# An expert loop one step shorter, with the last item's rows summed in by one-hot products

## The reference

```python
# 64 routed experts, the best 8 for each token, and one shared expert
gates = sel / jnp.sum(sel, axis=-1, keepdims=True) * ROUTED_SCALE
...
h = jax.nn.silu(xb @ w_gate[e]) * (xb @ w_up[e])
y = (h @ w_down[e]) * g[:, None]
return acc.at[tok].add(y), None
...
x = layer_norm(DEEPNORM_ALPHA * x + ffn, ln2_g[l], ln2_b[l])
```

## Time and profile before

| what | value |
|---|---|
| median of 3 runs | 1369.25 us (1366.78 to 1371.58) |
| the profiled execution | 1365.46 us, span 1363.9 us |
| PE busy | 1293.6 us, 95% of the span |
| DVE, ACT, POOL busy | 954.3, 792.3, 483.7 us |
| DMA | 324.11 MB, mean 238 GB/s |
| chain, by engine | PE 81%, DVE 8%, DMA 5%, issue 2%, ACT 2%, POOL 1% |

### The profile page before, as it was taken

The page is one execution under the profiler, slowest core; times in us unless marked ns, Lnnn a source line. Parts: engine busy times, 40 slices in busy tenths (PEclk is TensorE's granted clock), DMA queues, the critical chain, the costliest instruction groups (busy, mean ns, idle before and its releaser), DMA issues.

```text
span 1363.9 us, 25482 instructions
## 1 busy us (share of the span) xinstructions
PE 1293.6 (95%) x6257; PEld 1069.0 (78%) x6258; DVE 954.3 (70%) x1115; ACT 792.3 (58%) x1045; POOL 483.7 (35%) x441
## 2 busy tenths in 40 slices
PE   7989888899989999999999999999999999999966
PEld 6877776788867888888888888888888888888852
DVE  5989977766664958575796456646669579777737
ACT  4122266222255959575786556656678678676724
POOL 0000115366553334334344334334334343333422
PEclk9999879899998999999999999999999999999998
DMA  6121304232569999897999698869889899999747
GB/s 250 47 93 47 144 11 139 89 90 79 160 197 336 356 327 309 301 281 247 338 343 350 211 260 276 264 193 306 286 270 368 249 335 338 339 328 305 216 121 306
DMA packets 78065, 324.11 MB, mean 238 GB/s; under 512 B 22656, under 2 KB 24864, under 8 KB 52816
## 3 DMA queue, kind: packets, MB, share of 16 engines
q1 hardware_dynamic: 43152, 251.05, 49.1%
q0 software_dynamic: 33728, 68.47, 21.4%
q10 hardware_dynamic: 1152, 4.19, 0.8%
HBM read 290.51 MB, written 67.72 MB: 263 GB/s over the span
## 4 chain that ended last, share of the span: by engine, by line
PE 81%; DVE 8%; DMA 5%; issue 2%; ACT 2%; POOL 1%; ACTq 0%; POOLq 0%; SPq 0%; DVEq 0%
PE ps L1813 37%; PE ps L1831 18%; PE ps L1550 6%; PE ps L1678 5%; PE ps L1586 4%; DMA raw<-in_w_up 3%; PE ps L1757 2%; PE ps L1564 2%; DVE cv L1118 2%; PE ps L1844 1%; PE ps L1669 1%; PE ps L1598 1%; PE ps L1642 1%; POOL list_d L600 1%; PE ps L1745 1%
## 5 line engine op out<-in xcount | busy, mean ns | idle before, releaser
L1813 PE MATMUL ps<-wgu,xTe 128*128 x2304 | 548.8, 394 | 3.8 <-issue 2.5
L1813 PEld LDWEIGHTS ps<-wgu,xTe 128*128 128x128 f32 x2304 | 425.7, 188 | 90.7 <-issue 5.8
L653 POOL DMA_INDIRECT sum_d<-ysb,idx x95 | 177.7, 1870 | 508.5 <-ACT ysb L918 438.6
L1831 PE MATMUL ps<-wdn,hT 128*128 (+1 forms) x1236 | 299.3, 391 | 0.0
L1421 DVE TENSOR_TENSOR wgu<-raw,wgu (+1 forms) x128 | 287.7, 2289 | 6.0 <-issue 2.3
L1831 PEld LDWEIGHTS ps<-wdn,hT 128*128 128x128 f32 x1236 | 232.3, 189 | 48.3 <-DVE wdn L1354 0.2
L841 ACT CAST wgu<-raw (+1 forms) x128 | 246.8, 1929 | 3.1 <-SPq L450 2.5
L1426 DVE TENSOR_TENSOR xTe<-ps,xTe 128x512 fp32r<-128x512 f32 x194 | 124.6, 684 | 138.0 <-ACT xTe L910 138.0
L918 ACT ACTIVATE ysb<-ps,idx 128x512 f32<-128x512 f32 x188 | 119.1, 685 | 122.6 <-PE ps L1831 122.6
L1421 DVE TENSOR_TENSOR wdn<-raw,wdn x64 | 146.7, 2293 | 59.5 <-ACT wdn L903 59.1
L643 POOL DMA_INDIRECT xg<-x_d,idx x99 | 110.1, 1113 | 45.1 <-issue 34.3
(11 more groups left out here) (231 smaller groups left out, 1185.3 us busy)
## 6 DMA issues: line engine op xcount, KB each, us to landing
raw<-in_w_gate SPq DMA_DIRECT2D x64, 1024.0 KB, 11.4
raw<-in_w_up SPq DMA_DIRECT2D x64, 1024.0 KB, 8.4
raw<-in_w_down SPq DMA_DIRECT2D x64, 1024.0 KB, 9.4
wraw<-in_w_in SPq DMA_DIRECT2D x10, 512.0 KB, 3.4
xin<-in_xt SPq DMA_DIRECT2D x8, 512.0 KB, 7.6
wraw<-in_w_kv SPq DMA_DIRECT2D x8, 512.0 KB, 3.3
wor<-in_w_out SPq DMA_DIRECT2D x4, 1024.0 KB, 7.9
xres<-in_x SPq DMA_DIRECT2D x8, 512.0 KB, 4.9
```

The costliest lines, as they stand in the source:

```text
L653: g.indirect_dma_start(out=sums, out_offset=bass.IndirectOffsetOnAxis(ap=idx[:, c % RING, c % 2:c % 2 + 1], axis=0), in_=ysb[:, c % 2], in ...
L1813: last = mm(ps[:, 2 + s, :], xTe[:, s, st, d], wgu[:, w, mo, d].rearrange("p a n -> p (a n)"), start=(d == 0 and st == 0 and mo == 0), sto ...
L1831: last = mm(ps[:, down_bank(i) + h, :], hT[:, s, st, c], wdn[:, w, mo, c, h * 512:(h + 1) * 512].rearrange("p a n -> p (a n)"), start=(c = ...
```

## The change

The loop ends one step earlier on every engine. The last item's down product is done behind the loop, into PSUM banks 0 and 1, after a copy of its hidden rows (`hl`), two transposes, a cast and a split that the loop's last step did before. The item before the last is still scattered, the last is not: its scaled rows go to `yl` in SBUF. VectorE builds `sel`, for each tile a 128 by 128 matrix with a one where the last item's row belongs to that tile's token, and TensorE adds `sel` times `yl` to each tile. All eight tiles are now summed in PSUM, each from three parts (early, `yl`, late); tiles 0 and 4 (renamed `BN`) still get their moments on VectorE, now from PSUM. Early and late swap: the early sum is the even items', complete without the last item's scatter. It is loaded in two transfers of four tiles, once all remaining scatters but the last have landed; the late sum is loaded in eight transfers after the last remaining scatter.

```diff
             sp.wait_ge(s_tabs, 1)
+            n_items = sp.value_load(nit[0:1, 0:1], min_val=NT + E, max_val=MAX_ITEMS)
             past = sp.value_load(nit[0:1, 1:2], min_val=E, max_val=MAX_ITEMS - NT)
             late = sp.value_load(nit[0:1, 2:3], min_val=E - 2, max_val=MAX_ITEMS - NT - 2)
...
-            for t in range(2):
-                load_early(t, s_early)
-            sp.wait_ge(s_endC, 3)
-            sp.wait_ge(s_endR, 1)
+            sp.wait_ge(s_yd[0], 16 * ((late + 1) // 2))
+            sp.wait_ge(s_yd[1], 16 * (late // 2))
+            sp.sem_inc(s_seen, 1)
+            for n in range(2):
+                sp.dma_start(early[:, 4 * n:4 * n + 4], rows_of((past + 1) % 2, 4 * n, 4)).then_inc(s_early[n], 16)
+            sp.wait_ge(s_yd[0], 16 * (past // 2))
+            sp.wait_ge(s_yd[1], 16 * ((late + 1) // 2))
+            sp.wait_ge(s_gu, n_items)
+            sp.sem_inc(s_seen, 1)
             for t in range(NT):
-                if t >= 2:
-                    load_early(t, s_late[t])
-                load_late(t)
+                sp.dma_start(late_[:, t:t + 1], rows_of(past % 2, t, 1)).then_inc(s_late[t], 16)
...
+            g.iota(iotaR[:], pattern=[[1, 128]], base=0, channel_multiplier=0,
+                   allow_small_or_imprecise_dtypes=True).then_inc(s_pt2, 1)
+            g.iota(off8[:], pattern=[[128, NT]], base=0, channel_multiplier=0,
+                   allow_small_or_imprecise_dtypes=True).then_inc(s_pt2, 1)
...
+            act.wait_ge(s_dn, late + (NT + 1))
+            act.wait_ge(s_ht, n_items)
+            nc.scalar.copy(hT[:, 0, 0], ps[:, 4, 0:256].rearrange("p (c n) -> p c n", c=2)).then_inc(s_hhi, 1)
...
+            act.wait_ge(s_yd[0], 16 * (late // 2))
+            act.wait_ge(s_yd[1], 16 * (before // 2))
+            slot = n_items % 2
+            for b in range(2):
+                nc.scalar.activation(ysb[:, bass.ds(slot, 1), b * 512:(b + 1) * 512].rearrange("p a n -> p (a n)"),
+                                     ps[:, 5 + b, :], ACT.Copy, scale=gate_of(2)).then_inc(s_y, 1)
             act.wait_ge(s_dn, n_items)
+            nc.scalar.activation(yl[:, 0:512], ps[:, 0, :], ACT.Copy, scale=gate_of(1)).then_inc(s_yl, 1)
...
+            v.wait_ge(s_h, n_items)
+            V.tensor_copy(hl[:], hx[:, bass.ds((n_items + 1) % 2, 1)].rearrange("p a n -> p (a n)")).then_inc(s_sel, 1)
+            v.wait_ge(s_hhi, n_items)
+            V.tensor_tensor(hT[:, 0, 1], ps[:, 4, 0:256].rearrange("p (c n) -> p c n", c=2),
+                            hT[:, 0, 0].bitcast(F), ALU.subtract).then_inc(s_hlo, 1)
...
+            V.tensor_tensor(sel[:], iotaR[:].unsqueeze(1).to_broadcast([128, NT, 128]),
+                            tok8[:].unsqueeze(2).to_broadcast([128, NT, 128]), ALU.is_equal).then_inc(s_sel, 1)
             v.wait_ge(s_dn, n_items)
...
+            V.tensor_scalar(yl[:, 512:D], ps[:, 1, :], gate, None, ALU.mult).then_inc(s_yl, 1)
...
             for t in range(NT):
-                if t + 2 in ADDED:
-                    add(t + 2)
-                if t + 1 in ADDED:
+                if t + 1 in BN:
                     moments(t + 1)
                 normalise(t)
...
-                        with pe.If(n_items > 2 * jj + NT - 1):
+                        with pe.If(n_items > 2 * jj + NT):
                             step_pe(2 * jj + NT, 0, jj + 1)
...
+            pe.wait_ge(s_sel, 1)
+            for c in range(2):
+                last = nc.tensor.transpose(ps[:, 4, c * 128:(c + 1) * 128],
+                                           hl[:, c * 128:(c + 1) * 128], ident[:])
...
+            def add_part(t, first, rows):
+                lhs = sel[:, t] if rows is yl else ident[:]
                 for h in range(2):
+                    cols = slice(h * 512, (h + 1) * 512)
+                    last = mm(ps[:, sum_bank(t) + h, :], lhs, yl[:, cols] if rows is yl else rows[:, t, cols],
+                              start=first, stop=(rows is late_))
                 return last
...
+            pe.wait_ge(s_early[0], 16)
+            add_part(0, True, early)
+            pe.wait_ge(s_y, 2 * n_items)
+            add_part(1, True, early)
+            add_part(2, True, early)
+            pe.wait_ge(s_sel, 2)
+            pe.wait_ge(s_yl, 2)
+            for t in range(3):
+                add_part(t, False, yl)
+            add_part(3, True, early)
+            add_part(3, False, yl)
+            for t in range(NT):
                 if t >= 4:
+                    if t == 4:
+                        pe.wait_ge(s_early[1], 16)
                     pe.wait_ge(s_acc, t - 3)
+                    add_part(t, True, early)
+                    add_part(t, False, yl)
+                pe.wait_ge(s_late[t], 16)
+                add_part(t, False, late_).then_inc(s_pc, 1)
```

More of the change, by code:

```diff
@@ L975, in _ @@
                 step_act(i, i % 2, 0)
+            late = act.value_load(nit[0:1, 2:3], min_val=E - 2, max_val=MAX_ITEMS - NT - 2)
+            before = act.value_load(nit[0:1, 3:4], min_val=E - 3, max_val=MAX_ITEMS - NT - 3)
             with act.Fori(0, GROUPS) as group:
-                with act.If(n_items > 2 * GROUP * group + NT + 3):
+                with act.If(n_items > 2 * GROUP * group + NT + 4):
                     with act.Fori(0, GROUP) as pair:
                         jj = GROUP * group + pair
-                        with act.If(n_items > 2 * jj + NT + 3):
+                        with act.If(n_items > 2 * jj + NT + 4):
@@ L981, in _ @@
                             step_act(2 * jj + NT + 4, 0, jj + 1)
-                            with act.If(n_items > 2 * jj + NT + 4):
+                            with act.If(n_items > 2 * jj + NT + 5):
                                 step_act(2 * jj + NT + 5, 1, jj + 1)
[L986 to L989, removed]
@@ L1414, in item_tables_out @@
                 step(V.tensor_scalar(nit[0:1, 1:2], endE[0:1, NE - 1:NE], float(NT), None, ALU.subtract))
-                step(V.tensor_scalar(nit[0:1, 2:3], endE[0:1, NE - 1:NE], float(NT + 2), None, ALU.subtract))
+                for n in (2, 3):
+                    step(V.tensor_scalar(nit[0:1, n:n + 1], endE[0:1, NE - 1:NE], float(NT + n), None, ALU.subtract))
                 settle()
@@ L1481, in _ @@
                             step_v(2 * jj + NT, 0)
-                            with v.If(n_items > 2 * jj + NT):
+                            with v.If(n_items > 2 * jj + NT + 1):
                                 step_v(2 * jj + NT + 1, 1)
-            settle()
-            v.wait_ge(s_h, n_items + 1)
-            v.wait_ge(s_yd[0], 16 * ((late + 1) // 2))
-            v.wait_ge(s_yd[1], 16 * (late // 2))
-            v.wait_ge(s_dn, n_items)
-            gate = idx[:, bass.ds((n_items + RING - 1) % RING, 1), 2:3].bitcast(F).rearrange("p a n -> p (a n)")
@@ new lines, in _ @@
+            settle()
+            v.wait_ge(s_pt2, 11)
+            last = bass.ds((n_items + RING - 1) % RING, 1)
+            step(V.tensor_copy(tok1[:], idx[:, last, 0:1].rearrange("p a n -> p (a n)")))
+            settle()
+            step(V.tensor_scalar(tok8[:], off8[:], tok1[:, 0:1], -1.0, ALU.subtract, ALU.mult))
+            settle()
+            V.tensor_tensor(sel[:], iotaR[:].unsqueeze(1).to_broadcast([128, NT, 128]),
+                            tok8[:].unsqueeze(2).to_broadcast([128, NT, 128]), ALU.is_equal).then_inc(s_sel, 1)
@@ L1894, in _ @@
[L1894 to L1897, removed]
+            pe.wait_ge(s_sel, 1)
+            for c in range(2):
+                last = nc.tensor.transpose(ps[:, 4, c * 128:(c + 1) * 128],
+                                           hl[:, c * 128:(c + 1) * 128], ident[:])
+            last.then_inc(s_ht, 1)
+            pe.wait_ge(s_elo, n_items + 1)
+            pe.wait_ge(s_dhi, NE)
@@ new lines, in _ @@
+            pe.wait_ge(s_hhi, n_items)
+            for st, mo in ((0, 0), (1, 0), (0, 1)):
+                if st == 1:
+                    pe.wait_ge(s_hlo, n_items)
+                if mo == 1:
+                    pe.wait_ge(s_dlo, NE)
+                for h in range(2):
+                    for c in range(2):
+                        last = mm(ps[:, h, :], hT[:, 0, st, c], wdn[:, E % 2, mo, c, h * 512:(h + 1) * 512],
+                                  start=(c == 0 and st == 0 and mo == 0), stop=(c == 1 and mo == 1))
@@ new lines, in _ @@
+            last.then_inc(s_dn, 1)
+            def add_part(t, first, rows):
+                lhs = sel[:, t] if rows is yl else ident[:]
+                for h in range(2):
+                    cols = slice(h * 512, (h + 1) * 512)
+                    last = mm(ps[:, sum_bank(t) + h, :], lhs, yl[:, cols] if rows is yl else rows[:, t, cols],
+                              start=first, stop=(rows is late_))
+                return last
+            pe.wait_ge(s_early[0], 16)
+            add_part(0, True, early)
```

93 lines of the change are left out of this document (35 added, 58 removed).

## The result

The changed kernel takes 1372.94 us (median of 20 runs, 1367.34 to 1377.83), the kernel before 1367.27 us in runs beside it (20 runs, 1360.79 to 1372.49). The ratio is 1.0039, with a 95% interval of 1.0027 to 1.0051: by that ratio it is slower by 5.3 us, between 3.7 and 7.0. The forecast was 4.5 us.

What follows compares the result with a forecast made beforehand. TensorE's 24 parts behind the early load bound the new end: 1315.8 + 41.3 + 1.7 + 0.16 + 2.9 + 0.64 + 2.8 + 3.1 = 1368.4 against 1363.9, 4.5 us slower. Median 1373.8; range 1369 to 1378, forecast's own 1372 to 1378.

Steps and rivals of the forecast that it cites:

- the stretch: From the end of the loop's last down product to the end of the span; 57.5 us in the kernel before.
- The shorter loop: End of loop: last down product ends at about 1311, where it ended at 1315.68; 4.7 us gained, not 9.3.
- Issue of the early load and start of the scatter: Behind the loop: SP issues the early load at 1308.0; POOL starts the last remaining scatter at 1310.6.
- Its landing: First half of the early sums, four tiles, there at 1315.8; bounds 1314.3 without sharing, 1317.2 with the whole scatter ahead.
- The scatter's share: Early load beside the last scatter's data: gets about half the engines, so 1.5 us were added.
- the start-up of 1.2 us: Early load: 3.7 us from issue to landing of a pair of 0.5 MB loads, less 2.55 us of moving.
- The parts: TensorE's summing behind the early load: 24 parts of 1.72 us, 41.3 us; eight stand before the first late part.
- The clock: TensorE's first four products after its idle wait run at half speed: 1.7 us more, bounds 0 and 3.4.
- The end: After the last part, one tile's norm and store: ScalarE 2.9, POOL's power 0.64, VectorE 2.8, store 3.1 us.
- Slack where it was seen: Late loads through by about 1333, ahead of the sums; additions in the loop nothing to 1.6 us, taken as nothing.
- that within 0.3%: Rival: same order, but scatter leaves the early load alone or clock stays up; +3.0, +2.8, both +1.3; chance 0.35.
- The rival on the faster side: Rival: late rows, there at 1323, set the summing stage's pace, not TensorE; end at 1356.4, 7.5 us earlier; chance 0.07.

## Why the prediction was right, and where its terms were off

The sign, the size and the mechanism held: TensorE's 24 parts behind one load bound the new end, and 4.5 us lies in the measured interval of 3.7 to 7.0. Against the one profiled execution the sum was 2.4 us short: it made the stretch 62.0 us (1306.41 to 1368.4), and it was 64.4. That the forecast lies within a microsecond of the timed 5.3 us is thus in part luck, as the sum was made for the stretch, and that grew by 6.9.

- **The shorter loop.** The last down product was to end 4.6 us after the loop's last one; it ended 4.25 us after (1314.59).
- **Issue of the early load and start of the scatter.** Predicted 1.6 and 4.2 us after the loop's end, measured 1.49 and 3.53.
- **Its landing: mis-sized.** Predicted 7.8 us from issue, measured 9.64. The scatter's share was right, 1.5 us, and so was the stream: with the scatter held, this load alone moves 2.06 MB between 1311 and 1316, 0.41 MB/us. Wrong was "The norm weights ahead of it in SP's queue, 1.05 MB, are through about when it starts": moving them gave 0.7 us. Wrong was also the start-up of 1.2 us. It was read from the 3.7 us of the earlier trace rows, as if both loads of the pair were there by then; but that is the middle of two loads, each counted from its own issue. The landings of the pair (least, median, most), and SP's queue from 1311 to 1316 with the scatter held:

```profile
DMA to landing us min/median/max: 3.3/3.7/4.0
...
q1 hardware_dynamic: 518, 2.06, 102.4%
```

A load of 0.52 MB, 1.3 us by the earlier trace rows, was thus there after 3.3 us: 2.0 us of start-up, 0.8 more than in the sum. If the terms add up, 0.3 us stays open (9.64 − 2.0 − 5.1 − 1.5 − 0.7). By the Trainium skill's 358 GB/s for a core's HBM (DMA: Bandwidth & Descriptors, Specifications) the first half would need, by an estimate, 0.8 us more than the prediction's 5.1; the 2.06 MB in 5 us, 412 GB/s, do not agree with that.
- **The parts.** 1.72 us each, eight of them ahead of the first late part: right, and the largest term.
- **The clock: mis-sized.** Four products at half speed, 1.7 us, were predicted; 2.3 us were lost, within the bounds of 0 to 3.4.
- **The end.** From the last part to the end of the span 9.44 us (1365.26 to 1374.7), as the sum had it: 2.9 + 0.64 + 2.8 + 3.1.
- **Slack where it was seen.** The late loads are issued from 1325.05 on, and TensorE asks for the first at 1337.63 without waiting. VectorE's and ScalarE's added work, and that in the loop, cost nothing that can be measured: the timed difference from the kernel before is within 3 us of that of the stretch in each of these kernels (−7.5 beside −4.6 without the third part, −7.2 beside −8.0 with the late rows first, 5.3 beside 6.9 for the change), mostly on the cheaper side, so no loss hides in the loop.

The two mis-sized terms, 1.8 and 0.6 us, make the 2.4. Of the rivals, that within 0.3% falls by its conditions: the clock fell and the scatter did share. The rival on the faster side falls too: its condition was a part under 1.26 us, and the parts took 1.72. Where the condition is nearly met it comes near: with a cheaper third part and the early sums by tile, TensorE does wait for late rows, and tiles then pass 3.90 us apart, a mean of 1.30 us for a part. Timeline, TensorE, late rows first:

```profile
1340.96 1.88 PE L1922 MATMUL ps<-late__126,ident 128*128 128x512 f32 x4
...
1344.86 1.88 PE L1922 MATMUL ps<-late__126,ident 128*128 128x512 f32 x4
```

## What to carry to other kernels

Work that is moved from a transfer to an engine is free only if that engine has room at that point: count what then stands in its queue behind the wait, and compare that time with the pace of the stage. A load that starts a queue of work should come in pieces that release the first work item early; the idle time that it saves can save the clock too. Once the engine is relieved, the next transfer is the wait, so loads are ordered by when their rows are needed, not by when they become available.

## What was not expected of the hardware

- The scatter took 10.9 us to land beside the early load, 6.1 in the earlier trace rows and 6.1 again where the load was through first; it delayed the early load by 1.5 us and was itself delayed by nearly 5. Issues with us to landing, changed kernel:

```profile
early<-sum_d SPq DMA_DIRECT2D x2, 2048.0 KB, 12.7
...
sum_d<-ysb,idx POOLq DMA_INDIRECT x1, 10.9
```

- Idle times of 2.67, 3.68, 5.30, 5.37, 5.41, 6.82 and 6.92 us (twelve overwritten products, norm weights behind four early tiles, norm weights behind the early load, scatter held, cheaper one-hot parts, no third part, changed kernel) were each followed by products at 1.2 GHz; those of 0.50, 1.01 and 1.98 us by products at 2.4 GHz. The loss did not follow the idle time: 1.6 us behind 2.67 us (43.05 − 41.47), 2.9 behind 5.37 (44.40 − 41.47), 2.3 behind 6.92.
- The time at which an unaltered loop ends varies by over 4 us from one profiled execution to the next. Spans of two single profiles can't be subtracted to learn what a change at the end is worth; stretches from a common point can, to about 1 us: the end of the kernel before took 57.5 us, and 56.6 in the kernel with the additions to the loop (1305.53 to 1362.1), which leaves that end as it was.
